# High and low halves of weights in pairs, and masked attention units in 128 + 256 columns

## The reference

```python
x = x + concatenate([out_a, out_b, out_c]) @ w_out          # outa, outb
x = x + softmax(q k^T * 128**-0.5) v @ xattn_wo             # xq, cross, xo
x = x + square(relu(h @ w_up)) @ w_down                     # up, down
mix = (gate_gla * y_gla + gate_pool * y_pool) @ w_out       # gout, pout, out2
x = layer_norm(ALPHA * x + gt_m * mix)
x = layer_norm(ALPHA * x + gt_f * (silu(gate) * up) @ w_ffn_out)   # fin, fout
```

## Time and profile before

| | |
|---|---|
| median of 3 executions | 3023.03 us (3022.83 to 3024.53) |
| the profiled execution's own time | 3025.02 us |
| its span in the profile | 3023.7 us |
| busy share: PE, PEld, DVE, ACT | 97%, 84%, 72%, 48% |
| chain that ended last, by engine | PE 91%, DVE 5%, ACT 2%, issue 1%, DMA 1% |
| chain by line | 513 50%, 518 26%, 554, 556 and 561 3% each |
| granted TensorE clock over the span | 0.989 |
| HBM | 214 GB/s |

### The profile page before, as it was taken

One profiled execution on the slowest core, in us unless ns is written; L12 is line 12 of the kernel. 1 busy time (PEld: TensorE's weight loads), 2 busy tenths in 40 slices (PEclk: granted clock), 3 DMA queues, 4 the chain that ended last, 5 costly groups with the idle time before them and its releaser, 6 DMA issues.

```text
span 3023.7 us, 40090 instructions
## 1 busy us (share of the span) xinstructions
PE 2941.7 (97%) x16526; PEld 2545.6 (84%) x16526; DVE 2170.4 (72%) x2677; ACT 1454.5 (48%) x1941; POOL 8.5 (0%) x21
## 2 busy tenths in 40 slices
PE   8999999999999999998999999999999999999998
PEld 7888788888888888887887778888878888888886
DVE  5556767889899886789756656558888775555557
ACT  5445555544444444555444444544545444444444
POOL 0000000000000000000000000000000000000000
PEclk9999999999999999999999999999999999999999
DMA  6545234677677785577655445559646765555553
GB/s 251 194 168 195 98 140 151 233 263 260 257 264 265 288 316 208 183 273 273 257 185 181 167 163 190 192 216 344 226 160 251 280 249 183 193 183 193 185 191 112
DMA packets 107237, 648.61 MB, mean 215 GB/s; under 512 B 11920, under 2 KB 11920, under 8 KB 43440
## 3 DMA queue, kind: packets, MB, share of 16 engines
q1 hardware_dynamic: 99936, 621.86, 56.7%
q10 hardware_dynamic: 5184, 16.78, 1.4%
q0 software_dynamic: 1936, 7.41, 0.6%
HBM read 635.52 MB, written 10.49 MB: 214 GB/s over the span
## 4 chain that ended last, share of the span: by engine, by line
PE 91%; DVE 5%; ACT 2%; issue 1%; DMA 1%; SPq 0%; DVEq 0%; ACTq 0%
PE PS L513 50%; PE PS L518 26%; PE PS L554 3%; PE PS L556 3%; PE PS L561 3%; DVE RL L2036 1%; PE PS L791 1%; ACT RH L1194 1%; PE PS L1058 1%; PE PS L930 0%; PE PS L1045 0%; DMA RW<-in_w_ckv 0%; PE PS L976 0%; PE PS L582 0%; PE PS L693 0%
## 5 line engine op out<-in xcount | busy, mean ns | idle before, releaser
L2036 DVE TENSOR_TENSOR RL<-RW,RH 128x1024 fp32r<-128x1024 f32 x974 | 1177.9, 1222 | 544.7 <-ACT RH L1194 538.7
L1194 ACT ACTIVATE RH<-RW 128x1024 fp32r<-128x1024 f32 x974 | 1015.5, 1055 | 768.6 <-PE PS L518 652.0
L513 PE MATMUL PS<-A,RH 128*128 128x512 f32 x4544 | 1162.8, 398 | 35.0 <-ACT RH L1194 10.3
L513 PEld LDWEIGHTS PS<-A,RH 128*128 128x128 f32 x4544 | 827.1, 191 | 193.9 <-issue 37.8
L518 PEld LDWEIGHTS PS<-A,RL 128*128 128x128 f32 x4544 | 624.9, 192 | 45.4
L518 PE MATMUL PS<-A,RL 128*128 128x256 f32 x4544 | 637.9, 284 | 0.0
L513 PE MATMUL PS<-H,RH 128*128 128x512 f32 x2304 | 582.1, 395 | 1.2 <-ACT RH L1194 1.2
L513 PEld LDWEIGHTS PS<-H,RH 128*128 128x128 f32 x2304 | 416.2, 189 | 76.7 <-issue 1.4
L518 PEld LDWEIGHTS PS<-H,RL 128*128 128x128 f32 x2304 | 314.5, 190 | 22.7
L518 PE MATMUL PS<-H,RL 128*128 128x256 f32 x2304 | 321.3, 282 | 0.0
L1201 ACT ACTIVATE LT<-PS 128x512 f32<-128x512 f32 x232 | 138.2, 596 | 326.4 <-PE PS L518 326.3
(11 more groups left out here) (253 smaller groups left out, 1511.6 us busy)
## 6 DMA issues: line engine op xcount, KB each, us to landing
RW<-in_w_fin SPq DMA_DIRECT2D x88, 1024.0 KB, 4.8
G<-in_w_ada SPq DMA_DIRECT2D x160, 512.0 KB, 5.9
RW<-in_w_up SPq DMA_DIRECT2D x64, 1024.0 KB, 4.9
RW<-in_w_down SPq DMA_DIRECT2D x64, 1024.0 KB, 5.2
RW<-in_w_fout SPq DMA_DIRECT2D x44, 1024.0 KB, 4.7
RW<-in_w_v SPq DMA_DIRECT2D x32, 1024.0 KB, 4.9
RW<-in_w_bg SPq DMA_DIRECT2D x32, 1024.0 KB, 4.8
RW<-in_w_k SPq DMA_DIRECT2D x16, 1024.0 KB, 5.0
```

Source lines behind the costliest of these rows:

```text
L513: t.matmul(pair[mm][:, :], wh[:, k, mm * 128:mm * 128 + 128], x2(4 * c + k)[0], start=first and k == 0, stop=False, skip_group_check=True)
L1194: a.activation(m.high(x), m.slot(j)[:, x % 2 * HC:x % 2 * HC + HC], ACT.Copy).then_inc(s["hi"], 1)
L2036: v.tensor_tensor(m.low(x), m.slot(j)[:, x % 2 * HC:x % 2 * HC + HC], m.high(x).bitcast(F32), ALU.subtract).then_inc(s["lo"], 1)
```

## The change

Two things at once.

**Pairs.** `gemm` gets a flag `paired`. With it PE runs the high products of two halves, then the low products of the same two. It is set for outb, up, down, g2, pout, fin, fout and out2 (eight products, 308 chunks). Each half's high products now signal `hused`, in all products, and ACT waits, before it writes half x, for the high products of half x-5 and for DVE's low part of it, and no more for its low products.

**Masked units.** Scores, mask, exponentials and product take 128 columns for the first 128 queries and 256 for the second. One DVE operation per part adds the mask to the scores, multiplies by minus the scale and takes the minimum along the row; the exponential's scale is -1. The mask's logarithms are divided by the scale. The bank is freed by the exponentials, not by the first DVE operation. The broadcast multiply becomes two with a column as the scalar. The constants' masks are 384 columns wide, not 512.

```diff
@@ -234,6 +234,11 @@
         pass
+
+
+def widths(n, causal):
+
+    return (P, 2 * P) if n == 2 * P and causal else (n, n)
@@ -491,33 +496,51 @@
-    def gemm(blocks, halves, x2, need, zipped=False, beside=None):
+    def gemm(blocks, halves, x2, need, zipped=False, beside=None, paired=False):
...
         num.block += blocks
-        for b, c in steps(blocks, halves, zipped):
-            n = num.half
-            num.half += 1
+
+        def high(n, b, c):
+
             if c == 0:
...
             wh = m.high(n).rearrange("p (k n) -> p k n", k=4)
-            wl = m.low(n).rearrange("p (k n) -> p k n", k=4)
-            first, last = c == 0, c == halves - 1
             pair = m.banks[2 * ((g0 + b) % 2):2 * ((g0 + b) % 2) + 2]
...
                 for mm in range(2):
-                    t.matmul(pair[mm][:, :], wh[:, k, mm * 128:mm * 128 + 128], x2(4 * c + k)[0], start=first and k == 0,
-                             stop=False, skip_group_check=True)
+                    done = t.matmul(pair[mm][:, :], wh[:, k, mm * 128:mm * 128 + 128], x2(4 * c + k)[0],
+                                    start=c == 0 and k == 0, stop=False, skip_group_check=True)
+            done.then_inc(s["hused"], 1)
+
+        def low(n, b, c):
+
             t.wait_ge(s["lo"], n + 1)
+            wl = m.low(n).rearrange("p (k n) -> p k n", k=4)
+            pair = m.banks[2 * ((g0 + b) % 2):2 * ((g0 + b) % 2) + 2]
             for k in range(4):
...
                     done = t.matmul(pair[mm][:, 0:256], wl[:, k, mm * 128:mm * 128 + 128], x2(4 * c + k)[1], start=False,
-                                    stop=last and k == 3, skip_group_check=True)
+                                    stop=c == halves - 1 and k == 3, skip_group_check=True)
             done.then_inc(s["used"], 1)
+
+        order = steps(blocks, halves, zipped)
+        for x, (b, c) in enumerate(order):
+            n = num.half
+            num.half += 1
+            last = c == halves - 1
+            if not paired:
+                high(n, b, c)
+                low(n, b, c)
+            elif x % 2 == 0:
+                high(n, b, c)
+                high(n + 1, *order[x + 1])
+                low(n, b, c)
+                low(n + 1, *order[x + 1])
             if rest is not None:
@@ -553,8 +576,9 @@
                                  skip_group_check=True)
-                        t.matmul(out[mm], lo(2 * c + k)[:, rows[mm]], wh[:, k, :], start=False, stop=False,
-                                 skip_group_check=True)
+                        done = t.matmul(out[mm], lo(2 * c + k)[:, rows[mm]], wh[:, k, :], start=False, stop=False,
+                                        skip_group_check=True)
+                done.then_inc(s["hused"], 1)
                 t.wait_ge(s["lo"], n + 1)
@@ -579,8 +603,9 @@
             for k in range(8):
-                t.matmul(bk.ap[:, :], wh[:, k, :], A2(8 * half + k)[0], start=half == k == 0, stop=False,
-                         skip_group_check=True)
+                done = t.matmul(bk.ap[:, :], wh[:, k, :], A2(8 * half + k)[0], start=half == k == 0, stop=False,
+                                skip_group_check=True)
+            done.then_inc(s["hused"], 1)
             t.wait_ge(s["lo"], n + 1)
@@ -750,14 +775,15 @@
-    def scores(qT, kT, n=256):
+    def scores(qT, kT, n=256, causal=True):
         u, bk = att["unit"], banks.next()
+        w = widths(n, causal)
         att["unit"] += 1
...
         wait_empty(bk)
-        t.matmul(bk.ap[:, 0:n], qT[:, 0:128], kT, start=True, stop=True)
-        t.matmul(bk.ap[:, n:2 * n], qT[:, 128:256], kT, start=True, stop=True).then_inc(bk.full, 1)
+        t.matmul(bk.ap[:, 0:w[0]], qT[:, 0:128], kT[:, 0:w[0]], start=True, stop=True)
+        t.matmul(bk.ap[:, w[0]:w[0] + w[1]], qT[:, 128:256], kT, start=True, stop=True).then_inc(bk.full, 1)
         return u, sc
@@ -772,8 +798,8 @@
         blocks = [(0, 0), (1, 0), (1, 1)] if causal else [(0, 0), (0, 1), (1, 0), (1, 1)]
-        for j, (i, k) in enumerate(blocks):
-            done = t.transpose(bk.ap[:, j * 128:j * 128 + 128], sc[:, i * 256 + k * 128:i * 256 + k * 128 + 128], ident)
+        for j in range(len(blocks)):
+            done = t.transpose(bk.ap[:, j * 128:j * 128 + 128], sc[:, j * 128:j * 128 + 128], ident)
         done.then_inc(bk.full, 1)
@@ -873,7 +899,7 @@
-    L.outb = lambda: gemm(8, 2, twin(m.A, 8), mix_of(4))
+    L.outb = lambda: gemm(8, 2, twin(m.A, 8), mix_of(4), paired=True)
     L.fed_rest = lambda: None
@@ -885,7 +911,7 @@
             if k < 4:
-                unit[k] = scores(m.XQ[:, k * 256:k * 256 + 256], m.XK[:, k * 256:k * 256 + 256])
+                unit[k] = scores(m.XQ[:, k * 256:k * 256 + 256], m.XK[:, k * 256:k * 256 + 256], causal=False)
             if 2 <= k < 6:
@@ -932,10 +958,10 @@
         first = q == b0 == 0
-        yield from gemm(2 * nb, 4, A2, fed(2) if first else nothing, zipped=first)
+        yield from gemm(2 * nb, 4, A2, fed(2) if first else nothing, zipped=first, paired=True)
     def down(q):
-        yield from gemm(8, 4, twin(m.H, 16 * q, 24), lambda c: t.wait_ge(s["ul"], 8 * q + c + 1))
+        yield from gemm(8, 4, twin(m.H, 16 * q, 24), lambda c: t.wait_ge(s["ul"], 8 * q + c + 1), paired=True)
@@ -1115,9 +1141,9 @@
     L.p2, L.pool = p2, pool
-    L.g2 = lambda: gemm(8, 4, A2, nothing)
+    L.g2 = lambda: gemm(8, 4, A2, nothing, paired=True)
     L.gout = lambda: gemm(8, 4, H2, lambda c: t.wait_ge(s["gl"], c + 1))
-    L.pout = lambda: gemm(8, 2, A2, lambda c: t.wait_ge(s["pl"], c + 1))
+    L.pout = lambda: gemm(8, 2, A2, lambda c: t.wait_ge(s["pl"], c + 1), paired=True)
     L.cp_loads = lambda: idle(12)
@@ -1163,13 +1189,13 @@
         first = b0 == 0
-        yield from gemm(2 * nb, 4, A2, (lambda c: t.wait_ge(s["fl2"], c + 1)) if first else nothing, zipped=first)
+        yield from gemm(2 * nb, 4, A2, (lambda c: t.wait_ge(s["fl2"], c + 1)) if first else nothing, zipped=first, paired=True)
...
         yield from gemm(8, n // 4, twin(m.H, first, 24), lambda c: t.wait_ge(s["fgl"], first // 2 + c + 1),
-                        beside=normed(1) if part == 2 else None)
-
-    L.out2 = lambda: gemm(8, 4, H2, lambda c: t.wait_ge(s["ml2"], 17 + c), beside=normed(0))
+                        beside=normed(1) if part == 2 else None, paired=True)
+
+    L.out2 = lambda: gemm(8, 4, H2, lambda c: t.wait_ge(s["ml2"], 17 + c), beside=normed(0), paired=True)
     L.modulated_ffn, L.fin, L.fout = modulated_ffn, fin, fout
@@ -1190,7 +1216,8 @@
             if x >= NR:
-                a.wait_ge(s["used"], x - NR + 1)
+                a.wait_ge(s["lo"], x - NR + 1)
+                a.wait_ge(s["hused"], x - NR + 1)
             a.activation(m.high(x), m.slot(j)[:, x % 2 * HC:x % 2 * HC + HC], ACT.Copy).then_inc(s["hi"], 1)
@@ -1437,11 +1464,12 @@
         a.wait_ge(s["mx"], u + 1)
-        src, scale, done = (bk.ap, SCALE, bk.empty) if direct else (sc, 1.0, s["ex"])
+        src, scale = (bk.ap, SCALE) if direct else (sc, -1.0)
+        w = widths(n, not direct)
         for i in range(2):
-            x = a.activation(sc[:, i * n:i * n + n], src[:, i * n:i * n + n], ACT.Exp, bias=sm[:, i:i + 1],
-                             scale=scale, accum_out=sm[:, 2 + i:3 + i])
-        x.then_inc(done, 1)
+            d = slice(i * w[0], i * w[0] + w[i])
+            x = a.activation(sc[:, d], src[:, d], ACT.Exp, bias=sm[:, i:i + 1], scale=scale, accum_out=sm[:, 2 + i:3 + i])
+        x.then_inc(bk.empty, 1)
@@ -2281,11 +2309,11 @@
         if bias is not None:
-            v.scalar_tensor_tensor(sc[:, 0:2 * n], bk.ap[:, 0:2 * n], SCALE, bias, ALU.mult,
-                                   ALU.add).then_inc(bk.empty, 1)
-            v.wait_ge(bk.empty, bk.n)
-            v.tensor_reduce(sm[:, 0:2], sc[:, 0:2 * n].rearrange("p (i k) -> p i k", i=2), AX, ALU.max,
-                            negate=True).then_inc(s["mx"], 1)
+            w = widths(n, True)
+            for i in range(2):
+                d = slice(i * w[0], i * w[0] + w[i])
+                r = v.tensor_tensor_reduce(sc[:, d], bk.ap[:, d], bias[:, d], -SCALE, 3e38, ALU.add, ALU.min, sm[:, i:i + 1])
+            r.then_inc(s["mx"], 1)
         else:
@@ -2296,17 +2324,16 @@
         sc, sm = m.bufs[at], m.sms[(1 + u) % 8]
-        sv = sc[:, 0:2 * n].rearrange("p (i k) -> p i k", i=2)
-        if direct:
-            v.wait_ge(bk.empty, bk.n)
-        else:
-            v.wait_ge(s["ex"], u + 1)
+        w = widths(n, not direct)
+        v.wait_ge(bk.empty, bk.n)
         stepped(v.reciprocal(sm[:, 4:6], sm[:, 2:4]))
...
         wait_step()
-        p = v.tensor_tensor(sv, sv, sm[:, 4:6].unsqueeze(2).to_broadcast([P, 2, n]), ALU.mult)
+        for i in range(2):
+            d = slice(i * w[0], i * w[0] + w[i])
+            p = v.tensor_scalar(sc[:, d], sc[:, d], sm[:, 4 + i:5 + i], None, ALU.mult)
         if valid is not None:
@@ -3370,12 +3397,13 @@
              + ((dist >= 0) & (dist % 16 == 0) & (dist // 16 <= 128)))
```

(11 more changed lines are left out.)

## The result

The changed kernel takes 3006.12 us (median; 3004.02 to 3009.94), the kernel before, run beside it, 3023.78 (3022.83 to 3026.64). The ratio is 0.9944 with an interval of 0.9931 to 0.9956: 17.7 us faster, where the sum of the forecast was 25.7 (2998 us, range 2988 to 3014). The profiled execution has a span of 3008.6 us, 15.1 less than the one of the earlier trace rows.

The account below looks back on a forecast made before the run. The matrix engine, busy 2941.7 of 3023.7 us, was the bound, so time could come only from its pace, waits and clock. Terms summed to -25.7 us, from 3023.0 to 2997.3 by the median, stated as 2998; range 2988 to 3014.

Parts of the forecast that it names:

- Part 1, pairs: Paired products: 308 changes from narrow to wide fall away at 0.027 us each, 8.3 us, taken as -8.
- The first rival: Pair order brings nothing: debt belongs to the narrow steps, or 0.027 us has another source; 3005 us, 13%.
- Part 2, out2: Block 0's evacuation wait -2.1, the low clock behind it -1.5, block 6's sums behind the last half -1.7 us.
- Fout's last part: Three halves a block, so a pair spans block 0's end and the sum over X waits: +1.8 us.
- Fin's first pairs: First pairs want their second quarter of inputs 0.95 us sooner, where inputs are late: +0.9 us.
- The step of part 2 that failed: Conditioning vector's transposes up to one half later; vector engine's lead of 8 us covers it: 0, uncovered up to 2.8 each.
- Part 3, the ring: High ring freed at the end of the high products, so the scalar engine starts 0.95 us sooner: 0 by itself.
- Part 4, masked units: Twenty units of 256 columns: matrix engine -3.5, shorter unit chains cut two long nsa waits and clock falls, -11.6 us.
- the second I take for the same: Nsa's second long wait falls like the first, by 2.3 us, plus 3.5 from the low clock behind it.
- the second rival: Nsa's two long waits shrink by 1 us each but stay over 2 us, clock still falls: 3007 us, 20%.
- The slower cases: Score products in nsa wait for banks now freed by the second exponential: 3041 us, 5%; slower in all 0.06.
- over about 2 us can so be paid twice: Matrix engine's waits over about 2 us can cost again through the low clock behind them, as after 3.67 and 2.14.

Follow-up runs that it names:

- the fours: Changed kernel with the one masked operation on 256 + 256 columns, and g2 alone as four halves' high products, then their low ones: 3009.17 us, 0.995.
- both places mended: Against fewer pairs, the first down's last pair and the first pair of the up behind it as single chunks: 2999.05 us; run again, 2998.26.
- fewer pairs: Changed kernel, single halves for up's first part and each down (first eight), fin's first sixteen, all of fout's last part: 2997.86 us; run again, 3002.10.
- one pair apart: Changed kernel with the last pair of the first down alone taken as two single chunks: 3001.82 us, 0.9937.

## Why the prediction came out as it did

**Part 1, pairs: -8 forecast, -6.2 measured.** 308 joints (changes from narrow to wide) at 0.020, not 0.027. The reading of the debt was right, and the fours show that it hangs on the joint: half of the joints go, 0.32; half of the rest, 0.16. Too large was the term, because I took the narrow step for 0.12 whichever stood before it and resolved no gain there; the first narrow step after a wide run is some 0.007 shorter, by the products' starts, and that is lost with the joint. The Trainium skill, TensorE: Matmul & The Clock Gate, section Back-to-back issue gap, gives 518 cycles for 512 columns at 2.4 GHz, which is 216 ns, for a product by itself, with no term for the step before it. Here a wide product takes 227 ns within a long wide run, and g2's three lengths show that the step before counts. The first rival is out.

**Part 2, out2: -5.3 forecast; 107.22 to 101.24.** Less 16 joints (0.3), -5.7. Of this 2.1 hang on the new ring wait, since pairs with the old one take 103.31. The wait after block 0 and its low clock went, the sums of block 6 went behind the last half, and what was late next, the vector engine's chain, stands as the earlier trace rows had it with its wait cut from 2.60 to 0.88. Chain of waits, end of out2, after:
```profile
2231.41 1.93 PE PS L527 x16
2233.33 0.02 issue
2233.36 0.89 DVE X L2962 x2
...
2235.93 1.15 PE PS L1152 x4
```
**Fout's last part: +1.8 forecast, +1.9 measured** (1.62 in the stage, with 12 joints, 0.24, saved in it). Timeline, after, the sum over X of the earlier trace rows:
```profile
2933.36 1.10 PE L1152 MATMUL PS<-X,C 128*128 128x256 f32 x4 [1.70 <-DVE X L2962]
```
**Fin's first pairs: +0.9 forecast, +3.6 measured** (2.61 in the stage, with 48 joints, 1.0, saved in it). Timeline of the matrix engine where fin waits for its inputs, before and after:
```profile
2260.57 3.75 PE L513 MATMUL PS<-A,RH 128*128 128x512 f32 x8 [4.79 <-DVE A L2992]
2278.72 1.47 PE L513 MATMUL PS<-A,RH 128*128 128x512 f32 x5 [1.36 <-DVE A L2992]
```
```profile
2242.71 5.47 PE L516 MATMUL PS<-A,RH 128*128 128x512 f32 x16 [4.79 <-DVE A L3019]
...
2260.85 3.75 PE L516 MATMUL PS<-A,RH 128*128 128x512 f32 x8 [2.39 <-DVE A L3019]
```
From the first input to the last it is 18.15 us before and 18.14 after: the vector engine sets it. What differs is the work still to do then. A pair leaves the narrow run of the half before, 0.95 us, which is the +0.9 of the forecast. The other 2.7 are the clock, 1.00 before and 0.72 after: behind the wait the eight wide products take 3.75 us, where the eight at the same place before take 2.16 (2278.72 to 2280.88). The term left it out, though the forecast counted it everywhere else. The stretch, after:
```profile
2258.00:2270.00 12.00, 9.61 (x38) 7.97 (x38) 8.03 (x15) 5.51 (x10) 0.00 (x0) 0.72 0.25 94
```

**The step of part 2 that failed: "its lead is about three halves, so 0".** Transposes of the conditioning vector a half later cost 2.45 us in up and second down, 3.1 with the 0.64 saved in their joints; the price that I had given without cover was up to 2.8. Of the twelve places with transposes only one cost this, the one where the vector engine is so late that the matrix engine waits for it afterwards. The row of its waits for line 930, which I had not read, shows that at four of them there was no lead at all. It does not tell which one costs: before, the vector engine waited 0.85 us at 1134 us too; its waits there and at the group before grew by 4.4 us after, and that stretch lost nothing (the third down takes 91.13 before and 90.73 after, the up behind it 44.69 and 44.62).

**Part 3, the ring: 0 forecast, -5.4 in bg2** (5.5 with the ring alone). Up's first part shows nothing clear without pairs (136.35 with the new wait, 137.25 and 140.01 with the old one, and 135.9 to 141.1 over all kernels with the new one). I looked only at the waits for the high halves themselves. What gains is what the scalar engine does behind its ring wait; in bg2 that is the copy for which the matrix engine waits.

**Part 4, masked units: -15.1 forecast, -7.7 measured** (outa, xk and xv -7.0, qc -0.6). These are of one execution each: with the whole change of the units outa, xk and xv take 140.1 to 144.4 us, without it 150.7 to 151.5; qc takes 69.2 to 72.2 and 71.6 to 72.9. The kernel with the masked units alone, 8.1 us faster by the medians, says the same. The operations were sized right: 0.285 + 0.420 against 0.70, plus two reads of 0.083 less overlap; the exponential 0.402 and 0.494, forecast 0.39 and 0.50; the multiply in two a little over 0.1 shorter. The matrix engine's part is there: 0.21 a unit makes 0.63 for the three large units beside xv (36.07 to 35.44), and as much for the three beside xk (33.33 to 32.22), where a wait of 0.69 us on line 791 goes as well. What failed is "the second I take for the same". Timeline in nsa, after, against the earlier trace rows:
```profile
301.57 2.60 PE L817 MATMUL PS<-G 128*128 128x128 f32 x16 [1.48 <-ACT G L1487]
```
```profile
318.79 0.28 DVE L2315 CUSTOM_DVE_ANT_0 G<-PS,G 128x128 f32<-128x128 f32 x1
...
322.62 0.47 ACT L1487 ACTIVATE G<-PS 128x384 f32<-128x384 f32 x1
```
The first wait fell by 2.2, as forecast (2.3), and its clock fall went, in this execution. But the second was not its copy: it is the same lag, met again. From the end of the first wait the vector engine takes 18.3 us before and 17.2 after to that unit's mask, which stands behind the memory's norm; the matrix engine takes 20.1 and 16.6 to the second wait, since it ran at full clock. So 3.67 + 3.63 became 1.48 + 5.16, 0.7 less in all, and the clock fell behind the second alone: one of the forecast's signs of being wrong, a clock window that stays. The two waits here were for one late engine and so one debt: what the matrix engine saves between them it waits for at the second, unless the vector engine gains as much. The stretch behind the second wait, after:
```profile
321.00:331.00 10.00, 7.66 (x23) 6.18 (x24) 8.84 (x22) 7.15 (x16) 0.00 (x0) 0.50 0.14 57
```
**The sum.** The terms that were too large (part 4 by 7.4, part 1 by 1.8, fin by 2.7, the transposes by 3.1) come to 15.0, the one too small (part 3, 5.4) takes back a third, and the profiled execution's remaining 1 us is spread: the second product of v gives +1.8, up's first part and the first stages take some. That the time stands well inside the range is in part luck: without the ring's 5.4 us, for which the sum has no term, it would be some 3011.5, by the upper end. The time fell where the second rival, 3007, had it. Its mechanism is the nearer one too: a wait over 2 us stayed, though not for the reason it gave. The first rival's 3005 is as near, and g2 rules it out. The slower cases did not come; a score product of a masked unit never waited for its bank.

## What to carry to other kernels

When an order of work is changed for the matrix engine's sake, list every small group that rides between its runs (transposes, sums, copies) and read who already waits for it, and whether the matrix engine waits for that one in turn. A wait that stands already, as the 0.85 us here, says that there is no lead; it stood at two places, and cost time only where the waiting engine was the limit. When products are grouped, the ring's release has to be split with them, or the preparing engine loses more than the grouping brings (here 7.4 us slower than no pairs). Pair in the steady part, and leave single the first runs of a product whose inputs are just being made.

## What the runs showed of the hardware

**A fall of the clock can cost less the earlier it comes.** Nsa's code is the same in the changed kernel and in the one with both places mended, and the first wait is 1.48 us in both. In the latter's second run the clock fell behind it: the sixteen products take 3.84 us instead of 2.60, the matrix engine comes later to the second wait, which is 2.10 instead of 5.16, and outa, xk and xv take 140.05 instead of 143.63. Timeline of the matrix engine, that run:
```profile
297.50 3.84 PE L817 MATMUL PS<-G 128*128 128x128 f32 x16 [1.48 <-ACT G L1489]
319.27 2.60 PE L817 MATMUL PS<-G 128*128 128x128 f32 x16 [2.10 <-ACT G L1489]
```
The low clock lies where the vector engine is the limit and is so free, where behind a wait of 5.2 us it is paid in full. The 3.6 us between these two executions are that; the trace of fewer pairs shows the same as the second run (1.48, 2.08 and 140.07).

**The length of a wait didn't tell here whether the clock falls.** A wait of 2.14 us for the first score of the cross units is followed by 1.00 before (502 to 506 us) and by 0.72 after (494 to 500), and by 1.00 again (490 to 496) in the kernel with one pair apart, whose code there is that of after; one of 1.48 us is followed by a fall in one execution and by none in another. The forecast's "over about 2 us can so be paid twice" holds as "can" alone. Stretches as in the earlier trace rows, before, then after:
```profile
502.00:506.00 4.00, 2.82 (x12) 2.16 (x12) 2.54 (x7) 1.93 (x8) 0.00 (x0) 1.00 0.47 199
```
```profile
494.00:500.00 6.00, 5.81 (x20) 4.22 (x20) 3.74 (x13) 2.69 (x10) 0.00 (x0) 0.72 0.34 143
```
**The debt at a joint is paid in the first five wide steps.** By the starts of single products in fin, after, the gaps after a narrow run are 0.233, 0.236, 0.228, 0.233 and 0.231 us, and 0.227 from the sixth on. Why it is so stays open.
